# Reordered row tiles at the ends of the projection stage, nine expert widths, one 4 MB slot for the down weights

## What is computed

```python
h = rmsnorm(x);  q_lat, kv_lat, k_rope, pool_in, gates = split(h @ w_in)
y_attn = MLA(q_lat, kv_lat, k_rope) @ w_attn_out          # 8 heads, causal, QK norm, rotary part
y_pool = MultiScalePool(pool_in) @ w_pool_out             # trailing windows 2/4/8/16
x = x + (sigmoid(g_a) * y_attn + sigmoid(g_p) * y_pool) @ w_o
# MoE: top 4 of 32 experts for each token
logits = rmsnorm(x) @ w_router + b_router;  top_val, top_idx = top_k(logits, 4)
gu = x_e @ w_gate_up[e] + b_gate_up[e];  act = (up + 1) * gate * sigmoid(1.702 * gate)   # clamped
y_e = act @ w_down[e] + b_down[e];  x = x + sum(softmax(top_val) * y_e)
x = x + sigmoid(rmsnorm(x) @ w_ple_gate) * (p @ w_ple)
```

## Time and profile before

| | us |
|---|---|
| median of 3 runs | 2656.31 (2653.55 to 2656.97) |
| the profiled execution | 2656.76 |
| its span, first to last instruction | 2655.1 |
| PE busy | 2521.5 (95%) |
| DVE / ACT / POOL busy | 898.5 / 447.4 / 349.6 |

### The profile page before, as it was taken

The page is one execution under the profiler, slowest core; times in us unless marked ns, Lnnn a source line. Parts: engine busy times, 40 slices in busy tenths (PEclk is TensorE's granted clock), DMA queues, the critical chain, the costliest instruction groups (busy, mean ns, idle before and its releaser), DMA issues. The chain is left out here.

```text
span 2655.1 us, 46713 instructions
## 1 busy us (share of the span) xinstructions
PE 2521.5 (95%) x16704; PEld 2080.9 (78%) x16704; DVE 898.5 (34%) x2591; ACT 447.4 (17%) x1066; POOL 349.6 (13%) x553
## 2 busy tenths in 40 slices
PE   8998889999989679999999999999999999999599
PEld 6755665444435379999999999999999999999344
DVE  4743665000013522223233332333333333333353
ACT  3323443000001101111111111111111111111132
POOL 2530000000002211001001011010101111110220
PEclk9998999999999889999999999999999999999799
DMA  4000002210045457677778778888888888885441
GB/s 145 17 17 9 1 0 61 75 47 24 24 148 121 123 205 289 243 272 288 278 273 298 267 286 321 288 297 290 310 308 310 313 307 321 298 329 211 166 168 71
DMA packets 273895, 518.81 MB, mean 195 GB/s; under 512 B 14849, under 2 KB 54417, under 8 KB 273842
## 3 DMA queue, kind: packets, MB, share of 16 engines
q1 hardware_dynamic: 236946, 445.55, 48.0%
q0 software_dynamic: 17600, 38.97, 4.3%
q10 hardware_dynamic: 19296, 33.56, 3.5%
HBM read 484.34 MB, written 33.70 MB: 195 GB/s over the span
## 5 line engine op out<-in xcount | busy, mean ns | idle before, releaser
L1527 PE MATMUL bank<-arena_a,arena_w 128*128 128x128 f32 (+4 forms) x8192 | 978.6, 282 | 1.1 <-DVE arena_a L1624 1.1
L1527 PEld LDWEIGHTS bank<-arena_a,arena_w 128*128 128x128 f32 x8192 | 971.9, 191 | 1.5 <-issue 1.5
L1536 PE MATMUL bank<-arena_a,arena_w 128*128 128x128 f32 (+4 forms) x4096 | 512.1, 282 | 0.0
L1536 PEld LDWEIGHTS bank<-arena_a,arena_w 128*128 128x128 f32 x4096 | 497.1, 191 | 0.0
L1646 DVE TENSOR_SCALAR arena_m<-bank,arena_m 128x160 f32<-128x160 f32 x256 | 98.2, 383 | 591.4 <-PE bank L1527 591.4
L1020 PE MATMUL bank<-arena_h,arena_w 128*128 128x512 f32 x448 | 194.5, 592 | 0.0
L1602 ACT ACTIVATE arena_m<-arena_m 128x160 f32<-128x160 f32 x256 | 82.8, 335 | 623.9 <-DVE arena_m L1646 623.6
L1657 DVE TENSOR_SCALAR arena_m<-bank,arena_m 128x32 f32<-128x32 f32 x256 | 64.1, 250 | 342.4 <-PE bank L1536 326.0
L1020 PEld LDWEIGHTS bank<-arena_h,arena_w 128*128 128x128 f32 x448 | 85.1, 190 | 107.2 <-issue 107.2
L1440 POOL DMA_DIRECT2D arena_m<-slot_tokens x33 | 19.0, 576 | 1109.7 <-issue 1103.5
L1608 ACT ACTIVATE arena_a<-bank 128x512 f32<-128x512 f32 x64 | 38.2, 597 | 597.7 <-PE bank L1572 597.7
(11 more groups left out here) (289 smaller groups left out, 2221.4 us busy)
## 6 DMA issues: line engine op xcount, KB each, us to landing
arena_w<-in_w_gate_up_dram SPq DMA_DIRECT2D x124, 2048.0 KB
arena_w<-in_w_down_dram SPq DMA_DIRECT2D x62, 2048.0 KB, 12.4
expert_rows<-arena_a ACTq DMA_DIRECT2D x32, 512.0 KB
arena_a<-in_x_dram SPq DMA_DIRECT2D x16, 512.0 KB, 3.4
arena_w<-in_w_in_dram SPq DMA_DIRECT2D x16, 512.0 KB, 5.4
arena_w<-in_w_gate_up_dram ACTq DMA_DIRECT2D x4, 2048.0 KB
arena_w<-in_w_o_dram SPq DMA_DIRECT2D x1, 4096.0 KB, 16.1
arena_w<-in_w_down_dram ACTq DMA_DIRECT2D x2, 2048.0 KB, 21.2
```

The lines of the kernel that those rows point to most:

```text
L1527: m = pe.matmul(GU[f % 3][:, to:to + width], w[c][:, k, at:at + P], xT[:, k, 0:width], start=(k == 0), stop=(k == K - 1), skip_group_check ...
L1536: return pe.matmul(DN[d % 2][:, 0:width], wd[d // CT][:, k, at:at + P], actT[:, k, 0:width], start=(k == 0), stop=(k == KF - 1), skip_grou ...
```

## The change

1. **Widths.** `WIDTHS` gets nine entries, 160 to 128 in steps of 4, in place of five in steps of 8. The table of items has 12 fields for 8, and two tiles of DVE's sort move.
2. **Down weights.** One slot of 4 MB with one semaphore, loaded by one DMA when the whole down phase of the item before has been multiplied. In `route` ACT issues that one DMA in place of two.
3. **First row tile.** DVE does `turn(0)` and `scale(1)` ahead of `angles()`.
4. **Last row tile.** On DVE `windows(T - 3)` moves from ahead of `latent_turned(T - 2)` to ahead of `heads(T - 1)`, and `latent_turned(T - 1)` moves ahead of `heads(T - 2)`. On PE the last two channel groups of tile T - 2 move ahead of the bias transposes, and all channels of tile T - 1 ahead of `mix(T - 3)`. ACT's `keep_u` follow.
5. **Attention's begin.** POOL clears the old semaphores after its first `fetch`.

```diff
-WIDTHS = (160, 152, 144, 136, 128)
+WIDTHS = (160, 156, 152, 148, 144, 140, 136, 132, 128)
@@ front, PE
                         turn_latents(T - 1)
+                        pool_channels(T - 2, (2, 3))
                         pe.wait_ge(sem("biases"), 32)
...
                         heads(T - 1)
-                        pool_channels(T - 2, (2, 3))
+                        pool_channels(T - 1, (0, 1, 2, 3))
                         pe.wait_ge(sem("bias_dn"), 1)
                         mix(T - 3)
-                        pool_channels(T - 1, (0, 1, 2, 3))
@@ front, DVE
                         scale(0)
-                        angles()
                         for n in range(T):
                             turn(n)
+                            if n == 0:
+                                scale(1)
+                                angles()
                             if n >= 2:
                                 heads(n - 2)
-                            if n + 1 < T:
+                            if 0 < n < T - 1:
                                 scale(n + 1)
-                            if n >= 2:
+                            if 2 <= n < T - 1:
                                 windows(n - 2)
                             if n:
                                 latent_turned(n - 1)
                             latent(n)
+                        latent_turned(T - 1)
                         heads(T - 2)
-                        latent_turned(T - 1)
                         dve.wait_ge(sem("bias_psum"), 1)
                         dve.tensor_copy(bias_dn[:, :], MIX[:, 0:E * K]).then_inc(sem("bias_dn"), 1)
+                        windows(T - 3)
                         heads(T - 1)
@@ attend, POOL
-                        for s in front_sems[0].values():
-                            pool.sem_clear(s)
                         pool.memset(maskb[:, :], 0.0).then_inc(sem("c"), 1)
...
                         fetch(1, 1)
+                        for s in front_sems[0].values():
+                            pool.sem_clear(s)
@@ route, ACT
                         load_gate_up(act, 0, 1)
-                        for c in range(D // CW):
-                            load_down(act, 0, c)
+                        load_down(act, 0)
@@ experts, SP
-                            for c in range(D // CW):
-                                wait_value(sp, sem("dn_psum"), K * i + (CT * c + CT - K))
-                                load_down(sp, e, c)
+                            wait_value(sp, sem("dn_psum"), K * i)
+                            load_down(sp, e)
@@ experts, PE
-                            wait_value(pe, w_dn_here[0], 16 * i + 16)
+                            wait_value(pe, w_dn_here, 16 * i + 16)
...
-                                if d % CT == 0:
-                                    wait_value(pe, w_dn_here[d // CT], 16 * i + 16)
```

More of the change, by code:

```diff
@@ L559, in _ @@
                         head_norms(T - 2)
+                        keep_u(T - 2)
                         act.wait_ge(sem("bias_psum"), 1)
@@ L564, in _ @@
                         head_norms(T - 1)
-                        keep_u(T - 2)
+                        keep_u(T - 1)
                         keep_mix(T - 3)
-                        keep_u(T - 1)
                         act.wait_ge(sem("rotated"), T + 2)
@@ L1114, in route @@
                 lo = view(arena_h, 6084, 1)
-                bounds = view(arena_h, 6088, NW)
+                bounds = view(arena_h, 6128, NW)
                 ranked = view(arena_h, 6096, E)
                 wider = view(arena_a, 7168 + 3 * P, NW, E)
-                key, cls, oh, first, shift_e, nit = (view(arena_a, 7744 + E * j, E) for j in range(6))
+                key, cls, oh, first, shift_e, nit = (view(arena_a, 7840 + E * j, E) for j in range(6))
                 ahead, items_ahead = (view(arena_h, at, E, E) for at in (6144, 7168))
@@ L1414, in build @@
         wu = [view(arena_w, 2 * K * CW * c + K * CW, K, CW) for c in range(CH)]
-        wd = [view(arena_w, 2 * K * FF + KF * CW * c, KF, CW) for c in range(D // CW)]
+        wd = view(arena_w, 2 * K * FF, KF, D)
         w_gu_here = [top.enter_context(nc.semaphore(f"w_gu{c}")) for c in range(CH)]
-        w_dn_here = [top.enter_context(nc.semaphore(f"w_dn{c}")) for c in range(D // CW)]
+        w_dn_here = top.enter_context(nc.semaphore("w_dn"))
         def load_gate_up(eng, e, c):
@@ L1422, in load_gate_up, with load_down @@
                 eng.dma_start(w[c], w_gate_up[bass.ds(e, 1)][:, :, at:at + CW].rearrange("o (k p) n -> p (o k) n", p=P)).then_inc(w_gu_here[c], 16)
-        def load_down(eng, e, c):
-            eng.dma_start(wd[c], w_down[bass.ds(e, 1)][:, :, c * CW:(c + 1) * CW].rearrange("o (k p) n -> p (o k) n", p=P)).then_inc(w_dn_here[c], 16)
+        def load_down(eng, e):
+            eng.dma_start(wd, w_down[bass.ds(e, 1)].rearrange("o (k p) n -> p (o k) n", p=P)).then_inc(w_dn_here, 16)
         REST = WIDTH - P
@@ L1534, in part @@
                             def part(d, k):
-                                at = (d % CT) * P
-                                return pe.matmul(DN[d % 2][:, 0:width], wd[d // CT][:, k, at:at + P], actT[:, k, 0:width],
+                                return pe.matmul(DN[d % 2][:, 0:width], wd[:, k, d * P:(d + 1) * P], actT[:, k, 0:width],
                                                  start=(k == 0), stop=(k == KF - 1), skip_group_check=True)
-                            wait_value(pe, w_dn_here[0], 16 * i + 16)
+                            wait_value(pe, w_dn_here, 16 * i + 16)
                             for k in range(KF - 1):
```

## The result

The changed kernel took 2626.45 us (median, 2625.52 to 2627.96); beside it, on the same chip, the kernel before took 2654.93 (2652.92 to 2656.97). The ratio is 0.9892, 95% interval 0.9877 to 0.9907: 28.5 us or 1.1% less. The forecast was 2625.5 with 2618 to 2637 as its range. The profiled execution took 2625.52, with a span of 2623.9 us against 2655.1 before, so the traces differ by 31.2 us.

What follows compares the result with a forecast made beforehand. PE, busy 95% of the span, was taken as the bound: gains come from fewer or faster columns and less idle or low-clock time. 7.6 - 2.8 + 1.6 + 9.0 + 4.1 + 4.0 + 7.6 = 31.1 off 2656.8; forecast 2625.5 us, range 2618 to 2637.

Steps and rivals of the forecast that it cites:

- Widths: Experts' items: seven get 4 columns narrower, one 4 wider, 24 columns net at 0.316 us each; gain 7.6 us.
- the clock in route: Route's first tile: PE's clock stays up after a shorter pause, saving 1.7 us in logits and 2.0 in matmuls behind, 3.7.
- The rival of steps of eight: Experts: PE takes columns in eights, so 2.5 us lost in place of 7.6 won, 2635.5 us; chance 0.08.
- Nine reads: Experts: four more loop-end reads by PE from SBUF at 0.7 us each; cost 2.8 us, bounds 2.6 to 3.0.
- First tile: Front's first row tile: DVE's angles end later but its `latent(0)` starts at 24.6 for 26.18; gain 1.6 us.
- Last tile: Front's last row tile: PE waits of 2.2 and 4.2 us and 2.6 of low clock in heads go; gain 9.0 us.
- The clock's 4.0: Attention's begin: PE's clock stays up after a pause cut from 5.96 to about 1.9 us; gain 4.0, at most 7.7.
- the rival "the clock falls all the same": PE's clock falls after the shorter pauses too: attention's 4.0 us lost, route's 3.7, or both (2633 us); chance 0.30.
- Route: Route's first tile: 4.9 us from one down DMA fewer, 3.7 from the clock, less 1.0 for scatters; gain 7.6 us.
- the prediction's own sign ("if the clock is 0.5 after either pause"): Profile sign that the sum is wrong: low PE clock after the pause before attention (1.9 us) or in route (2.8).
- The scatters: Route: first scatter meets a loaded DMA and POOL's fetch, which PE needs, waits; cost 1.0 us, bounds 0 and 3.
- the slower rival: Experts: the 4 MB down load lands later than 29 us and PE waits in 31 items; 2718 us at 32; chance 0.03.

Runs made afterwards that it cites:

- the kernel with k halves: The changed kernel with its 4 MB down load as two DMAs, each half of the matrix's rows (512 rows of 4 KB): 2627.26 us, ratio 0.9901.
- the staggered loads: The changed kernel with ACT's two gate and up loads of route issued once the router weights have landed, down load unmoved: 2620.96 us, ratio 0.9882.

## Why the prediction came out

The median was met, and most of it for the reasons given; some sizes were off, in both directions, and one mechanism was wrong, the clock in route.

The sum began at 2656.8, of the profiled execution before. By the medians side by side the gain is 28.5 us, not the 31.1 of the sum; the traces differ by 31.2. Attention's clock (below) gave this pair 3.0 us more than it gives on average over the traces, and 31.2 - 3.0 = 28.2, an estimate, is near what the medians show.

*Widths.* As told: 45.53 us at 132, and 46.77 at 136, so four columns are a step and the floor lies below 132. The rival of steps of eight is refuted. The step from 132 to the 44.84 at 128 is 0.69 us, little more than half of the 1.24, so the floor is met at about 130 columns. The Trainium skill (TensorE: Matmul & The Clock Gate, LDWEIGHTS) gives a weight load as its columns / 1.2 ns, and the estimate made from it had the floor at 128: the 1.24 us agree with that, the 0.69 do not. From the second item on the items take 7.2 us less (1416.0 and 1408.8) for 7.6; the other 0.8 of the 8.0 is the first item's, whose low clock ended sooner.

*Nine reads.* They start 0.69 us apart on average, but the first is the longest, and the four added cost 0.64 each: 2.5 for 2.8. DVE's longer sort cost nothing, as put: it took 20.8 us for 19.3 and still ended 1.7 us before POOL's last gather.

*First tile.* 0.9 in this pair, about 1.5 over all traces, 1.6 forecast. The prediction had `scale(1)` wait for the second x tile, but took its landing as fixed: it varied by 1.4 us, and the new order passes that on, where the old one had a fixed start in both its traces.

*Last tile.* The terms were right and the sum 1 us short. The starts tell more than the bracketed idle times: with no wait between them PE's groups start 0.17 us before the last one's end, so the gaps that closed are 2.35 and 4.38. The slow heads gave 2.7 and L391 behind them 0.2 more, both at the low clock; the last 0.3, three steps of 0.1, are open.

*Attention.* The clears' 4.1 us are shown. The clock's 4.0 was in size too low for this pair (5.4) and in kind too sure: it was reckoned as if the length of the pause decided. Nine kernels here, the changed one among them, share this code and the 1.8 us pause. In five the clock stayed at 1.0; in four it fell, some 2 to 6 us after PE had begun again, and cost 0.9, 0.9, 2.5 and 4.6 us. With 5.96 us it fell in both traces and cost 5.4 and 1.3; with 0.93 in none of three. For attention the rival "the clock falls all the same" is thus true in a part of the executions. By these few traces the gain is on average 3.3 less 1.0, about 2.4 us. The Trainium skill (TensorE: Matmul & The Clock Gate, Part 4: PE-mode transpose) says that transposes don't count as busy the same way. By that rule, as the prediction took it, the clock falls here; the changed kernel's trace, with 1.00 through the sixteen of them and after, speaks against it as a rule.

*Route.* The mechanism, a fourth DMA whose rows had no room, was right: 14.25 us of issue became 9.21, the kernel with k halves and the queue's packets put it down to rows, and the staggered loads show that it is the rows still in the queue. The step that failed is the 3.7 us for a clock that stays up, which was set in full. It did not stay up: after a pause of 2.69 us the clock was low until 770 us, in the logits (2.26 for 1.87) and the matmuls behind (5.07 for 3.68), and only 2.0 of the 3.7 came, because the low clock was shorter and not because it was gone. Pauses of 2.6 to 3.0 us stand there in six kernels, the changed one among them, and it fell in all six; after the 1.10 us of the kernel with the clears first it did not. So in route the rival came true every time, by the prediction's own sign ("if the clock is 0.5 after either pause"), and 0.30 for one or both was too low. The trace before had held the warning: the prediction reckoned with pauses of 4.2 us and more, but PE entered route after 3.18 us of idle time, and the clock was low right behind it:

```profile
755.94 15.67 PE L1219 MATMUL bank<-arena_w,arena_m 128*128 128x512 f32 x32 [3.18 <-PEq L987]
```

```profile
758.00:761.00 3.00, 3.00 (x5) 1.20 (x4) 0.00 (x0) 0.00 (x0) 0.04 (x1) 0.58 0.79 292
```

The scatters cost 1.9 for 1.0. Together 5.2 for 7.6.

*Down slot in the experts.* Nothing won or lost, as said; with a landing of 15.2 us against 29 the slower rival never came near.

Route gave 2.4 us less than forecast, and attention's clock, the last tile and the items gave 2.8 more. That the median came within 1 us of the forecast is in part this cancelling, and in part luck: with a fourth run the median of the kernel before is 2654.93 in place of the 2656.31 that the forecast began from, and from there the same sum gives 2623.8, 2.6 us off.

## What to carry to other kernels

A DMA issue can hold up compute work on the same engine without any semaphore: count the rows already in that queue, and issue the loads as soon as the engine is idle, but behind the small loads that others wait for, and with time between them. A class of a work list that no item needs costs its entry and a wider item; take it out when the list always puts one in. And a gain that rests on the granted clock is to be given as a range over executions: one pair of traces showed 5.4 us where the average over many was less than half.

## What was not expected of the hardware

ACT's queue took two loads of 1024 rows of 2 KB each in 1.09 us, and the load behind them waited 6.0 to 9.5 us: 6.44 with 512 rows of 4 KB, 6.01 and 9.31 with 1024 rows of 2 KB, 7.61 to 9.47 with 1024 rows of 4 KB. The same load 8.4 us after the two took 0.38 us. That the rows count, and neither bytes nor the number of DMAs, follows from the sums and from the rows left when the wait ended; why one and the same load waited 6.01 us in one kernel and 9.31 in another is open.

The granted clock differs between executions of the same instructions. Behind the barrier between merge and route, PE pauses 3.18 us in every kernel; in twelve traces the clock was low behind it (15.67 us for the first 32 matmuls), in two it stayed up there (13.97). The Trainium skill (TensorE: Matmul & The Clock Gate, Part 1) says that the window in which the chip judges activity runs on by itself and does not restart with the kernel, which would let the same pause fall well or badly; no run here shows the window itself. What the traces do show is the price of a low clock: up to 5.4 us in attention's first head and 1.7 at the begin of route, enough to make up the 2.4 us by which the four executions of the changed kernel differ; that it does so is not shown, since only one of them was profiled.
